# Three stage joins of a long kernel: the rotation stage loads the selection stage's first keys and queries, and the last selection blocks load and partly split the output weights

## The reference

```
h     = rms_norm(x) * (1 + scale) + shift
proj  = h @ w_in                     # u_pool, g_pool, q, k, v, g_attn, qi, ki, wi
pool  = pool_mixer(u_pool) * silu(g_pool)          # windows 2, 4, 8, 16
q, k  = rope(rms_norm(q)), rope(rms_norm(k));  qi, ki = rope(qi), rope(ki)
for each block of 128 queries:
    score = sum_h relu(qi_h . ki) * wi_h           # 8 index heads, causal
    sel   = top 256 keys of score
    o     = softmax over sel of (q . k) @ v        # 8 heads, 2 key heads
out   = x + gate * (concat(pool, o * silu(g_attn)) @ w_out)
```

## Time and profile before

| | |
|---|---|
| median of 3 timed runs | 3430.47 us (3430.1 to 3436.8) |
| the profiled execution, its own time | 3433.9 us |
| its span in the trace | 3432.1 us |
| mean granted TensorE clock | 0.954 of full |
| PE, DVE, ACT busy | 3089.4, 2087.3, 1471.4 us |

### The profile page before, as it was taken

How to read it: one execution, slowest core, us unless ns; L and a number is a source line. 1 busy time by engine, 2 the same in 40 slices (tenths; PEclk the granted TensorE clock), 3 DMA queues, 4 the chain that set the end, 5 groups by cost and what they waited for, 6 DMA issues and landing times. The chain is left out here.

```text
span 3432.1 us, 47568 instructions
## 1 busy us (share of the span) xinstructions
PE 3089.4 (90%) x17524; PEld 2403.1 (70%) x17524; DVE 2087.3 (61%) x2938; ACT 1471.4 (43%) x2588; POOL 209.2 (6%) x473
## 2 busy tenths in 40 slices
PE   3999999989899998999988899999677889998599
PEld 3888788878688876777744677777456666776477
DVE  7777877743221117888859355324278888987343
ACT  6222322222211116777746123211178788888310
POOL 0000000000000000000011000000011111212000
PEclk6999999999999999999999899999878999999799
DMA  6222322246643322110054233322541111011375
GB/s 214 80 64 78 135 62 74 80 152 175 207 134 110 110 74 84 47 30 26 14 175 166 82 112 123 105 98 83 131 93 41 27 25 23 23 38 41 98 212 156
DMA packets 322034, 326.25 MB, mean 95 GB/s; under 512 B 40452, under 2 KB 272388, under 8 KB 314504
## 3 DMA queue, kind: packets, MB, share of 16 engines
q1 hardware_dynamic: 299464, 273.66, 26.9%
q0 software_dynamic: 7216, 42.01, 3.2%
q10 hardware_dynamic: 15136, 7.71, 0.8%
HBM read 205.22 MB, written 108.15 MB: 91 GB/s over the span
## 5 line engine op out<-in xcount | busy, mean ns | idle before, releaser
L535 PE MATMUL p_mx_ps<-s_h_a_hi,s_mx_w_hi 128*128 128x512 f32 x896 | 351.3, 392 | 25.9 <-DVE s_mx_w_lo L391 15.8
L535 PE MATMUL p_mx_ps<-s_h_a_lo,s_mx_w_hi 128*128 128x512 f32 x896 | 350.4, 391 | 0.0
L535 PE MATMUL p_mx_ps<-s_h_a_hi,s_mx_w_lo 128*128 128x512 f32 x896 | 350.1, 391 | 0.0
L1148 DVE TENSOR_TENSOR_SCAN s_st_prod<-s_st_soft,s_st_prod 128x512 f32<-128x512 f32 x192 | 234.6, 1267 | 19.0 <-ACT s_st_soft L1085 18.9
L1802 PE MATMUL p_pr_ps<-s_h_hi,s_pr_w_hi 128*128 128x512 f32 (+1 forms) x736 | 202.4, 397 | 21.7 <-DVE s_pr_w_lo L1687 13.1
L2578 PE MATMUL p_sa_turn<-s_ident,s_sa_arg 128*128 128x128 f32 x1088 | 167.3, 290 | 55.0 <-ACT s_sa_prob L2233 36.5
L535 PEld LDWEIGHTS p_mx_ps<-s_h_a_hi,s_mx_w_hi 128*128 128x128 f32 x896 | 169.3, 189 | 63.6 <-DVE s_mx_w_lo L391 20.6
L1085 ACT ACTIVATE s_st_soft<-p_st_z 128x512 f32<-128x512 f32 (+3 forms) x320 | 153.6, 533 | 115.7 <-PE p_st_z L1185 115.7
L1802 PE MATMUL p_pr_ps<-s_h_lo,s_pr_w_hi 128*128 128x512 f32 (+1 forms) x736 | 199.9, 394 | 0.0
L1802 PE MATMUL p_pr_ps<-s_h_hi,s_pr_w_lo 128*128 128x512 f32 (+1 forms) x736 | 198.8, 392 | 0.0
L535 PEld LDWEIGHTS p_mx_ps<-s_h_a_hi,s_mx_w_lo 128*128 128x128 f32 x896 | 169.3, 189 | 35.5
(11 more groups left out here) (302 smaller groups left out, 6675.8 us busy)
## 6 DMA issues: line engine op xcount, KB each, us to landing
s_mx_raw_first<-in_w_in_a SPq DMA_DIRECT2D x64, 256.0 KB, 3.9
s_mx_raw<-in_w_in_a SPq DMA_DIRECT2D x64, 256.0 KB, 3.8
d_kvqg_t<-s_pb_stage SPq DMA_DIRECT2D x16, 1024.0 KB, 5.1
s_pb_ada<-in_w_ada SPq DMA_DIRECT2D x16, 768.0 KB, 6.6
s_pr_raw<-in_w_in SPq DMA_DIRECT2D x22, 512.0 KB, 3.8
s_pr_work<-s_pr_stage SPq DMA_DIRECT2D x38, 256.0 KB, 4.7
d_rot_hi<-s_pr_rot POOLq DMA_DIRECT2D x9, 1024.0 KB, 4.2
d_rot_lo<-s_pr_stage POOLq DMA_DIRECT2D x9, 1024.0 KB, 6.2
```

Of the source, the lines that this page charges most:

```text
L535: ins = nc.tensor.matmul(bank[:], w[:, m, k, :], a[:, m, k, :], start=(k == 0 and n == 0), stop=(k == KH - 1 and n == 2))
L1148: nc.vector.tensor_tensor_scan(prod[:, b, s, 0:n][:, ::-1], back, back, carry, ALU.mult, ALU.bypass).then_inc(multiplied, 1)
```

## The change

Three stages get buffers in common (a class `AttentionSpace`), which lie where the earlier stage's buffers are dead. The last two `turn` blocks and pool 3 of the rotation stage move one place forward, so that two plain blocks stand last. Behind the stores of the last rotated block SP loads the selection stage's index weights, the first 1024 index keys, the first 128 attention keys, and queries of two index and two attention blocks. The selection stage's remaining keys come in other pieces (`KEY_PIECES`: attention 0 to 256, 256 to 1024, then 512 each; index 1024 to 1536, 1536 to 2048), and its first values are turned behind the first scores.

```diff
     for n in range(4):
         order += [("pool", ROW_U + P * n, P, n), ("turn", ROW_QI + P * n, P, None)]
-        order += [("plain", ROW_GA + P * n, P, None)] if n < 3 else []
-    order += [("turn", ROW_KI, TAIL, None), ("plain", ROW_GA + 3 * P, P, None)]
+        order += [("plain", ROW_GA + P * n, P, None)] if n < 2 else []
+    order += [("turn", ROW_KI, TAIL, None)] + [("plain", ROW_GA + P * n, P, None) for n in range(2, 4)]
...
+            last_turned = max(turned_rows)
+            sp.wait_ge(posted, posts[last_turned] + 1)
+            sp.wait_ge(mixed, WIDTHS)
+            for b in range(last_turned - 1, last_turned + 1):
+                sp.wait_ge(out_done[b % 2], 16 * outs_of[b])
+            for j in range(2):
+                sp.dma_start(space.wi_raw[j][:], p_t[ROW_WI:ROW_WI + IDX_HEADS, j * HALF:j * HALF + HALF]).then_inc(space.wi_in, 16)
+            load_queries(sp, space.qi_two, space.qi_in, FIRST_SELECTING, ROT_QI, rot_hi, rot_lo)
+            load_keys(sp, space, "index", 0, rot_hi, rot_lo)
+            load_queries(sp, space.q_two, space.q_in, 0, ROT_Q, rot_hi, rot_lo)
+            for g in range(KV_HEADS):
+                for half in range(2):
+                    for n, of in enumerate((rot_hi, rot_lo)):
+                        sp.dma_start(space.k_first[half * HD:half * HD + HD, n, g].bitcast(F32), of[ROT_K + HD * g:ROT_K + HD * g + HD, 0:P]).then_inc(space.k_first_in, 16)
+            load_queries(sp, space.qi_two, space.qi_in, FIRST_SELECTING + 1, ROT_QI, rot_hi, rot_lo)
+            load_queries(sp, space.q_two, space.q_in, 1, ROT_Q, rot_hi, rot_lo)
...
+    weights_at = {(14, 3): (0,), (15, 0): (1,)}
...
+            def load_weights(k):
+                sp.wait_ge(turned, 2 * unit_of[PAIRS * 12 - 1, len(parts(11)) - 1] + 2)
+                sp.dma_start(space.out_w_raw[k][:], w_out[k * P:k * P + P, :]).then_inc(space.out_w_in[k], 16)
...
+            for piece in range(2):
+                load_keys(sp, space, "attend", piece, rot_hi, rot_lo)
+            sp.wait_ge(wi_turned, 1)
+            for piece in range(2):
+                load_keys(sp, space, "index", 1 + piece, rot_hi, rot_lo)
+                if piece == 0:
+                    load_values(1)
+                load_keys(sp, space, "attend", 2 + piece, rot_hi, rot_lo)
...
+                for k in {13: (0, 1, 2, 3), 14: (4, 5, 6, 7)}.get(qb, ()):
+                    load_weights(k)
...
+            m_v, gp_v, ga_v = gated_rows(mix_t, p_t)
+            pool.wait_ge(masked, masks[LAST, 0, 0] + 1)
+            for t in range(2):
+                pool.wait_ge(o_out[ORDER.index(t) % 2], 16 * (ORDER.index(t) // 2 + 1))
+                pool.dma_start(space.out_m[:, t], m_v[t]).then_inc(space.out_m_in[t], 16)
+                pool.dma_start(space.out_g[:, t, 0:KC // 2], gp_v[t]).then_inc(space.out_m_in[t], 16)
+                pool.dma_start(space.out_g[:, t, KC // 2:], ga_v[t]).then_inc(space.out_m_in[t], 16)
...
-            act.dma_start(wi_raw, p_t[ROW_WI:ROW_WI + IDX_HEADS, :]).then_inc(w_in, 16)
+            def split_weights(k):
+                act.wait_ge(space.out_w_in[k], 16)
+                act.wait_ge(product, number["index", LAST, HEADS - 1, len(parts(LAST)) - 1] + 1)
+                nc.scalar.activation(space.out_w_hi[k][:], space.out_w_raw[k][:], ACT.Copy).then_inc(space.out_w_hi_done, 1)
...
                 if u < 0:
+                    leave_values(0)
                     continue
                 qb = block_of(u)
+                if units[u][1] == 0:
+                    for k in weights_at.get(divmod(units[u][0], PAIRS), ()):
+                        split_weights(k)
...
+            def split_weights(k):
+                dve.wait_ge(space.out_w_hi_done, k + 1)
+                nc.vector.tensor_tensor(space.out_w_lo[k][:], space.out_w_raw[k][:], space.out_w_hi[k][:].bitcast(F32), ALU.subtract).then_inc(space.out_w_lo_done, 1)
...
-            divide(TILES - 1)
+                if units[u][1] == 0:
+                    for k in weights_at.get(divmod(units[u][0], PAIRS), ()):
+                        split_weights(k)
+                if first_step(u, PAIRS - 1) and qb == LAST:
+                    for t in range(2):
+                        dve.wait_ge(space.out_m_in[t], 48)
+                        nc.vector.tensor_tensor(space.out_m[:, t], space.out_m[:, t], space.out_g[:, t], ALU.mult).then_inc(space.out_gated, 1)
+            for t in range(2):
+                dve.wait_ge(space.out_m_hi_done, t + 1)
+                nc.vector.tensor_tensor(space.out_m_lo[:, t], space.out_m[:, t], space.out_m_hi[:, t].bitcast(F32), ALU.subtract).then_inc(space.out_m_lo_done, 1)
```

```diff
+            with nc.allow_non_contiguous_dma(reason="one value of each query and head"):
+                sp.dma_start(inverse_t.rearrange("h q -> q h"), space.inverse[:]).then_inc(inverse_out, 16)
+            sp.dma_start(gate[:], gate_row.partition_broadcast(P)).then_inc(gate_in, 16)
+            sp.wait_ge(inverse_out, 16 * TILES)
+            for side in range(2):
+                sp.dma_start(space.spread[side * HD:side * HD + HD], inverse_t.rearrange("(c s) q -> s c q", s=2)[side].partition_broadcast(HD)).then_inc(spread_in, 16)
+            for j in range(DEEP):
+                sp.dma_start(xin[:, j], x_v[j]).then_inc(x_in[j], 16)
+            sp.wait_ge(divided, TILES)
+            sp.dma_start(o_v[ORDER[LAST]], space.o_sb[:, LAST % 2]).then_inc(o_out[LAST % 2], 16)
...
+            for k in range(EARLY, KC):
+                act.wait_ge(space.out_w_in[k], 16)
+                nc.scalar.activation(w_hi[k][:], w_raw[k][:], ACT.Copy).then_inc(w_hi_done, 1)
...
+            for k in range(EARLY, KC):
                 dve.wait_ge(w_hi_done, k + 1)
-                nc.vector.tensor_tensor(w_lo[:, k], w_raw[:, k % 2], w_hi[:, k].bitcast(F32), ALU.subtract).then_inc(w_lo_done, 1)
+                nc.vector.tensor_tensor(w_lo[k][:], w_raw[k][:], w_hi[k][:].bitcast(F32), ALU.subtract).then_inc(w_lo_done, 1)
+            dve.wait_ge(spread_in, 32 * TILES)
+            nc.vector.tensor_tensor(space.o_sb[:, LAST % 2].rearrange("p c n -> p (c n)"), space.o_ps[LAST % 2][:],
+                                    space.spread[:].rearrange("p c n -> p (c n)"), ALU.mult).then_inc(divided, 1)
             dve.wait_ge(gate_in, 16)
...
+            pe.wait_ge(m_lo_done, DEEP)
             for k in range(KC):
                 pe.wait_ge(w_lo_done, k + 1)
-                for j in range(2):
+                for t in range(DEEP):
                     for half in range(2):
                         cols = slice(half * 512, half * 512 + 512)
```

More of the change, by code:

```diff
@@ L2555, in scores @@
                 hi, lo = (ki_hi[:, of], ki_lo[:, of]) if kind == "index" else (k_hi[:, kv, of], k_lo[:, kv, of])
+                if kind == "attend" and qb == 0:
+                    hi, lo = (space.k_first[:, part, kv] for part in range(2))
                 nc.tensor.matmul(pr[n % BANKS][:, 0:width], q, hi, start=True, stop=False)
@@ L2603, in _ @@
                     scores(kind, qb, h, m)
+                if u < 0:
+                    turn_values(0)
                 if u >= 0:
@@ L2714, in _ @@
             dve.wait_ge(gate_in, 16)
-            with dve.Fori(0, PAIRS - 1) as i:
-                for j in range(2):
-                    finish(i * 2 + j, j)
-                    gates(i * 2 + (j + 2), j)
-            for j in range(2):
-                finish(TILES - 2 + j, j)
+            for t in range(LAST):
+                finish(t, 0, slice(0, DM))
+                if t + DEEP < TILES:
+                    split(t + DEEP)
+            for half in range(2):
+                finish(LAST, half, slice(half * 512, half * 512 + 512))
```

342 lines of the change are left out of this document (172 added, 170 removed).

## The result

The changed kernel takes 3396.4 us (median of 4 runs, 3392.8 to 3398.5) against 3430.3 before (4 runs): ratio 0.9896, 95% interval 0.9879 to 0.9913, so 34 us faster. The forecast was 3394, range 3384 to 3409. One of all the executions reported here, one of e5 (3640.3 us, at a granted clock of 0.839), was in a slower state of the chip and is left out of e5's median and ratio. The profiled execution took 3398.5 us, its span 3396.7, granted clock 0.958; before it was 3433.9 and 3432.1.

What follows compares the result with a forecast made beforehand. PE, 90% busy, was taken to bound the kernel, so only its idle stretches could go. Terms 15.5 + 19.8 + 1.3 = 36.6 us off the 3430.5 median gave 3394 us, own range 3390 to 3399, with rivals 3384 to 3409.

Steps and rivals of the forecast that it cites:

- (a): Rotation stage: the new order costs nothing, with 3.8 us of cover for pool 3; 22 loads are issued by 2453.
- a wait ahead of pool 3's mix: Rotation stage: a PE wait there would show the forecast of no cost for the new order wrong.
- (b): Start of selection stage: first relu at about S + 5.3 instead of S + 21.0; term 15.5 us.
- (c): End of selection stage: weight and tile loads delay block 14's inverse and division by +6 us, bounds 0 and +14.
- behind the weights alone it starts at 3199 (+4.4): End of selection stage: block 14's inverse store waits for weights 4 to 7 on its queue, 4.4 of the +6 us.
- a reload issued 14 to 15 us behind the store: End of selection stage: block 14's spread issued that long behind its inverse, not 8.6 us, would show the delay.
- (d): Slots (14,3) and (15,0): splits of weights 0 and 1 cost nothing; 2.3 us if DVE's idle time were gone.
- (e): Selection stage's end: output stage begins at 3221.8, PE at 3221.9 instead of 3241.71; term 19.8 us, 25.8 without delay.
- (f): Inside output stage: tile 2 starts at B + 30 as before, its load having 2.6 us of cover.
- (g): End of output stage: the last tile in halves gains 1.3 us; written-out loops cost nothing.
- 10.9 us for each later tile: Output stage: the time expected for each tile behind tile 2; if not met, the written-out loops would cost.
- R4: Output stage: written-out loops make PE wait for instructions, 54 ns a matmul eating the 36.6 us gain; chance 0.03.

Runs made afterwards that it cites:

- e5: Kernel before, with 32 bytes of filler ahead of the output stage's buffers, so all begin 32 bytes behind a multiple of 64; 3432.5 us, ratio 1.0006.
- e2: Changed kernel, with POOL's loads of output tiles 0 and 1 issued only behind the division of block 14; 3397.9 us.
- e4: Changed kernel, with the filler sa_pad cut from 32 to 24, putting the shared buffer at a multiple of 64 bytes; 3393.1 us.
- e3: Changed kernel, with output weights 0 to 3 and 4 to 7 each loaded one block earlier on SP's queue; 3397.3 us.
- e9: Changed kernel, with shared buffer at a multiple of 64 bytes and block 14's division behind the gating of tiles 0 and 1; 3388.6 us, ratio 0.9879.
- e6: Changed kernel, with POOL loading the rows of output tiles 0 and 1 one block earlier, behind block 14's first mask; 3397.8 us.
- e8: Changed kernel, with aligned buffers, tile loads one block earlier, and divisions of blocks 13 and 14 both in the next block's last pair; 3392.8 us.
- e12: Changed kernel, with weights 0 and 1 split at the output stage's start instead of in the selection stage's last slots; 3398.6 us.
- e1: Changed kernel, with the 22 early loads issued as the selection stage's first instructions instead of at the rotation stage's end; 3409.9 us, ratio 0.9937.
- e7: Changed kernel, with block 14's division moved in DVE's order to behind the gating of tiles 0 and 1; 3392.0 us, ratio 0.9885.
- e10: Kernel before, with both halves of the output weights 32 bytes behind a multiple of 64, the tiles' rows at a multiple; 3437.3 us, ratio 1.0016.

## Why the prediction was right, and where its terms were off

**(a) Rotation order: right.** The stage took the same time within 0.2 us: -1.5 at its first matmul, -1.6 at the next stage's start. The loads were issued 2437 to 2452, forecast 2439 to 2453. PE's waits in the stage are the same (8.6 us in four waits for ACT's copies both times), so the sign that I had set against it, a wait ahead of pool 3's mix, did not come. The order alone was not run.

**(b) Start of the selection stage: right.** The first relu came 4.1 us behind the start, where I had 5.3. The term of 15.5 also holds +0.5 and -0.7 behind that relu, so it is to be compared with both stretches together, 15.9. But that they agree so well is chance: the stretch behind the first relu took 706.0 us before, 707.0 here and 706.3, 705.5 and 706.2 in e2 to e4, so the 0.5 and the 0.7 can't be told from the scatter. Nor did PE wait for the fifth block's queries: from 2480 to 2560 us none of its waits ends with a DMA.

**(c) The delay of division 14: size right by luck, cause wrong.** +6 was forecast and +6.4 measured, but made of other parts. I had 4.4 us from the weights ahead on SP's queue, with the tile loads as an extra. The step that failed is "behind the weights alone it starts at 3199 (+4.4)". It rested on 298 GB/s, a rate of another stage; here each weight landed 5.2 us behind its issue, and in e2, with the same order on SP's queue, the store took 9.3 us, no more than the 8.6 to 10.5 of the last four blocks of the kernel before. e3 took the weights away and the delay stayed; e2 held the tile loads back and it was gone. I had also left the reload at its 4.4 us: in the changed kernel the store's share of the delay is 3.3 us (8.64 to 11.90 from its issue to that of the reload) and the reload's 3.2. The sign I had set, a reload issued 14 to 15 us behind the store, did not come: it was 11.9. This division into store and reload is not fixed: in e9 the store took 15.7 us and the reload 3.8, in e6 (block 13) 8.7 and 11.2. The sum is: with the tile loads over it, the division came 18.6 to 21.0 us behind the reciprocal in every kernel but e8, where it stood behind other work.

The Trainium skill ("DMA: Bandwidth & Descriptors", section "Queues, rings and completion order") has ring order within a queue and turns between rings, packet by packet. The first fits e8, where a store directly behind four weights took 12.2 us, over the 10.5 of the longest without either load; that the store and the weights share the DMA engines would fit as well. By the second the tile loads should cost the store only its turns, and the forecast took that for little. The traces show that the round trip beside these loads is 5.3 to 7.7 us longer than its 13.3 of before; that it is the turns that add up so is not shown.

**(d) Splits in the slots: right,** and e12 prices them: 2.3 us.

**(e) Start of the output stage: right.** Division 14 to first matmul fell by 26.4 us, forecast 25.8; the stage began at D + 7.6, forecast D + 8.4 (D: the time of division 14).

**(f) Inside it: right on tile 2.** The hole is 4.84 us and is ended by DVE, with no wait for a DMA. The load of tile 2 was issued 17.4 us behind the stage's start, forecast 17.5, though by compensation: the four terms that I named for it add up to 16.8, and the store was shorter than I had it (8.25 us, not 9.8) and the reload longer (5.95, not 3.6). The 1.0 us gained is the granted clock: 0.65 in the first 5 us and 1.00 behind them, where it was 0.50 and 0.93 before; e2 has 0.50 and 0.93 again, and 29.85 us.

**(g) and "10.9 us for each later tile": wrong.** The halves gave their 1.3 us (two half operations of 0.69 us end the work instead of two of 1.23), but each tile took 11.12 us: 13 x 0.24 = 3.1 us lost. I had moved the weights in my head without looking where they begin. R4 named the wrong reason for such a loss, the written-out loops: e4 has them too and runs at 10.88. Another 1.3 us, 0.24 of alignment in it, is the first of these tiles, tile 2, at a granted clock of 0.50 for 5 us behind the hole instead of 0.68: from its first matmul to DVE's first operation on it it took 14.13 us instead of 12.80. e2 and e3, with the same code there, had 0.70 and 0.71 and took 12.8 and 12.7. Of the other traces e1, e6, e7 and e8 took 13.9 to 14.1 and e10, a form of the kernel before, 13.9, so it is not the edit's; what decides it is not shown.

So the forecast of 3394 was 2 us low, nearly what the unlike operands cost. That it was no further off is luck in part: the span came out 1.2 us longer than forecast, since 4.7 us lost in (g) stand against 2.6 that the change did not earn, the 1.6 ahead of everything edited and the 1.0 of granted clock in (f). With aligned buffers e4 gave 3393.1.

## What to carry to other kernels

When a later stage's buffers are laid over dead ones, see that both operands of each matmul begin alike to a multiple of 64 bytes; here 32 bytes of filler cost 3 us of 34. When loads are moved forward under another stage's work, list the small round trips through memory that they will cross, stores and reloads of a few KB above all. The cure that paid was not to move the loads (e2, e6) but the one instruction that waits for the round trip, behind the work that doesn't need it (e7), and only as far as no other queue waits for it (e8). Moved so, it still waits for its round trip; what it no longer does is hold back other work.
